# A mixture-of-experts kernel: the last quad of each expert stage written out behind the loops, and its combination spread over four PSUM banks

## The reference

```python
for i in range(2):
    if i < 1: h = h + short_conv_mixer(rmsnorm(h, norm_mix_g[i]), ...)
    else:     h = h + mla_mixer(rmsnorm(h, norm_mix_g[i]), ..., *shared_kv_side(h, ...))
    h = h + hier_moe(rmsnorm(h, norm_ffn_g[i]), w_grp[i], w_exp[i], w_gate[i], w_up[i], w_down[i])
x = rmsnorm(h, final_norm_g)[:, 16:]
# second network: two layers of hgrn2 and sparse attention on x, each x = x + rmsnorm(y, post_norm)

def hier_moe(...):   # per token: the best of 8 groups, in it the best 2 of 8 experts, with weights
    hh = jax.nn.silu(xb @ w_gate[e]) * (xb @ w_up[e])      # 1024 -> 256
    return hh @ w_down[e]                                   # 256 -> 1024; times weight, summed over both
```

## Time and profile before

| | |
|---|---|
| median of 3 runs | 1847.31 us (1847.21 to 1848.0) |
| the profiled execution | 1850.71 us, its span 1848.9 us |
| TensorE busy | 1680.2 us (91%) |
| VectorE, ScalarE, GpSimd busy | 831.7, 653.1, 63.4 us |
| DMA | 526.4 MB, mean 285 GB/s |
| expert stage 0, stage 1 | first gate product at 138.6 and 750.3 us; last addition at 594 and 1206 us |

### The profile page before, as it was taken

The page is one execution under the profiler, slowest core; times in us unless marked ns, Lnnn a source line. Parts: engine busy times, 40 slices in busy tenths (PEclk is TensorE's granted clock), DMA queues, the critical chain, the costliest instruction groups (busy, mean ns, idle before and its releaser), DMA issues.

```text
span 1848.9 us, 31186 instructions
## 1 busy us (share of the span) xinstructions
PE 1680.2 (91%) x12410; PEld 1209.6 (65%) x12410; DVE 831.7 (45%) x1501; ACT 653.1 (35%) x1175; POOL 63.4 (3%) x58
## 2 busy tenths in 40 slices
PE   8999788887979999988887878999999999999997
PEld 8995434342435869534343433499998989999897
DVE  5652122121214754322121212279776646886663
ACT  4422111111103643211110111166557645655763
POOL 1100000000001000000000000010001110000110
PEclk9999888898989999999898889999999999999999
DMA  8669999999999324999999999935542243554232
GB/s 316 236 266 414 421 422 421 421 421 421 421 422 411 116 68 154 414 421 421 422 421 421 421 421 422 374 103 170 180 165 91 94 159 120 176 170 151 92 115 92
DMA packets 89224, 526.42 MB, mean 285 GB/s; under 512 B 10032, under 2 KB 10288, under 8 KB 39728
## 3 DMA queue, kind: packets, MB, share of 16 engines
q1 hardware_dynamic: 89136, 525.19, 72.2%
HBM read 524.10 MB, written 1.05 MB: 284 GB/s over the span
## 4 chain that ended last, share of the span: by engine, by line
PE 56%; DMA 28%; DVE 6%; SPq 6%; ACT 2%; issue 1%; DVEq 0%
DMA ring<-experts 16%; PE banks L504 13%; DMA arena<-experts 11%; PE banks L508 11%; PE banks L510 10%; PE banks L509 10%; SPq L443 6%; PE banks L702 5%; PE banks L684 3%; PE banks L720 3%; DVE arena L1606 1%; DVE hT L1731 1%; DMA ring<-dense 1%; PE banks L565 1%; ACT arena L1445 1%
## 5 line engine op out<-in xcount | busy, mean ns | idle before, releaser
L508 PE MATMUL banks<-arena_parts,ring_parts 128*128 128x256 f32 (+1 forms) x1444 | 418.3, 290 | 9.3 <-ACT arena L1157 5.1
L510 PE MATMUL banks<-arena_parts,ring_parts 128*128 128x256 f32 (+1 forms) x1444 | 409.9, 284 | 0.0
L509 PE MATMUL banks<-arena_parts,ring_parts 128*128 128x256 f32 (+1 forms) x1444 | 409.3, 283 | 0.0
L504 PEld LDWEIGHTS banks<-arena 128*128 128x128 f32 (+1 forms) x2512 | 302.4, 191 | 56.3 <-issue 43.9
L504 PE MATMUL banks<-arena 128*128 128x128 f32 (+3 forms) x2512 | 335.7, 288 | 1.9 <-ACT arena L1157 1.4
L702 PE MATMUL banks<-ring,arena 128*32 128x512 f32 x1536 | 237.2, 720 | 104.9 <-DMA ring<-experts 104.7
L1157 ACT ACTIVATE arena<-banks 128x256 f32<-128x256 f32 (+6 forms) x370 | 158.7, 455 | 396.4 <-PE banks L504 162.1
L1586 DVE TENSOR_TENSOR ring_parts<-ring,ring_parts 128x1024 fp32r<-128x1024 f32 x204 | 245.8, 1238 | 98.8 <-ACT ring_parts L1157 86.8
L508 PEld LDWEIGHTS banks<-arena_parts,ring_parts 128*128 128x128 f32 x1444 | 273.3, 189 | 17.8 <-issue 8.7
L1157 ACT ACTIVATE ring_parts<-ring 128x1024 fp32r<-128x1024 f32 x208 | 215.3, 1055 | 182.3 <-DMA ring<-dense 181.0
L509 PEld LDWEIGHTS banks<-arena_parts,ring_parts 128*128 128x128 f32 x1444 | 273.6, 189 | 0.3
(11 more groups left out here) (223 smaller groups left out, 1573.3 us busy)
## 6 DMA issues: line engine op xcount, KB each, us to landing
ring<-experts SPq DMA_DIRECT2D x192, 1024.0 KB, 26.5
arena<-experts SPq DMA_DIRECT2D x160, 1024.0 KB, 22.4
ring<-dense SPq DMA_DIRECT2D x224, 512.0 KB, 4.9
at<-experts SPq DMA_DIRECT2D x16, 1024.0 KB, 24.2
x<-experts SPq DMA_DIRECT2D x16, 1024.0 KB, 22.2
consts<-consts_in SPq DMA_DIRECT2D x1, 1414.0 KB, 13.0
vecs<-vecs_in SPq DMA_DIRECT2D x1, 1125.5 KB, 15.4
hT<-h_in SPq DMA_DIRECT2D x2, 544.0 KB, 4.4
```

The costliest lines, as they stand in the source:

```text
L504: return pe.matmul(o, lhsT, rhs, start=(k == 0), stop=(k == n - 1))
L508: pe.matmul(o, lhsT[0], rhs[0], start=(k == 0), stop=False)
L509: pe.matmul(o, lhsT[0], rhs[1], start=False, stop=False)
L510: return pe.matmul(o, lhsT[1], rhs[0], start=False, stop=(k == n - 1))
```

## The change

In both expert stages:

- TensorE's loop runs once less (7 pairs here) and the last pair of quads is written out behind it; ScalarE's and VectorE's loops run 15 times and the last quad is written out. The written-out last quad leaves out `prep(i + 2)`, `tokens(i + 2)` and `slots`.
- The combination behind the loops uses banks 6, 7, 0 and 1: product c waits for addition c - 4.
- In every combination the wait for VectorE's half of the output stands before the fifth product, no longer before the first.
- The counts that the loops read are one less; VectorE does two more operations on one value to make them.

SyncE's program is as before.

```diff
--- before.py
+++ after.py
@@ -217,7 +217,7 @@
         root = sb("root", [P, T])
         scalars = sb("scalars", [P, 3 + DC])
         eps, eps_root, eps_2, g_both = scalars[:, 0:1], scalars[:, 1:2], scalars[:, 2:3], scalars[:, 3:]
-        n_iter = sb("n_iter", [P, 4], I32)
+        n_but_one = sb("n_but_one", [P, 4], I32)
         small = {n: sb(f"{n}_bf16", [P, P], BF16) for n in ("ident", "ones", "upper", "mask")}
         chosen = sb("chosen", [P, TT, NE], BF16)
         n_last = sb("n_last", [P, 2], I32)
@@ -674,21 +674,23 @@
                         if c % 4 == 3:
                             m.then_inc(s["prep_done"], 1)
 
-                def combine(i):
+                def combine(i, banks=(6, 7)):
 
                     pe.wait_ge(s["ya_ready"], i + 1)
-                    pe.wait_ge(s["yd_ready"], i + 1)
                     pe.wait_ge(s["sw_ready"], i + 1)
                     for c in range(DC):
-                        pe.wait_ge(s["add_done"], i * DC + (c if c >= 2 else 1))
-                        pe.matmul(psum[:, 6 + c % 2, 0:T], mo_y[:, c * P:c * P + P], mo_sw[:, 0:T],
+                        if c == DC // 2:
+                            pe.wait_ge(s["yd_ready"], i + 1)
+                        pe.wait_ge(s["add_done"], i * DC + max(1, c + 2 - len(banks)))
+                        pe.matmul(psum[:, banks[c % len(banks)], 0:T], mo_y[:, c * P:c * P + P], mo_sw[:, 0:T],
                                   start=True, stop=True).then_inc(s["cmb_done"], 1)
 
                 prep(1)
                 pe.wait_ge(route["iter_ready"], layer + 1)
-                half = pe.value_load(n_iter[0:1, 2 + layer:3 + layer], min_val=QUADS // 2, max_val=QUADS * ROUNDS // 2)
-
-                def quad(i, odd):
+                pairs = pe.value_load(n_but_one[0:1, 2 + layer:3 + layer], min_val=QUADS // 2 - 1,
+                                      max_val=QUADS * ROUNDS // 2 - 1)
+
+                def quad(i, odd, last=False):
 
                     def weights(u):
                         pe.wait_ge(s[f"landed{u}"], i * 16 + 16)
@@ -702,7 +704,8 @@
                             m = pe.matmul(psum[32 * e:32 * e + 32, 3, :], mo_xs[:, k, 32 * e:32 * e + 32], w[:, e, :],
                                           start=(k == 0), stop=(k == 7), tile_position=(0, 32 * e))
                         m.then_inc(s["used"], 1)
-                    prep(i + 2)
+                    if not last:
+                        prep(i + 2)
                     pe.wait_ge(s["h_ready"], i + 1)
                     for k in range(2):
                         m = pe.transpose(psum[:, 3, k * P:k * P + P], mo_h[:, k * P:k * P + P], C("ident"))
@@ -721,10 +724,12 @@
                                               start=(k == 0), stop=(k == 1), tile_position=(0, 32 * e))
                             m.then_inc(s["used"], 1)
 
-                with pe.Fori(0, half) as pair:
+                with pe.Fori(0, pairs) as pair:
                     quad(pair * 2, False)
                     quad(pair * 2 + 1, True)
-                combine(half * 2)
+                quad(pairs * 2, False)
+                quad(pairs * 2 + 1, True, last=True)
+                combine(pairs * 2 + 2, (6, 7, 0, 1))
 
             def mla():
                 norm_sum(squares, DC, T, 5)
@@ -1226,19 +1231,25 @@
 
                 tokens(1)
                 act.wait_ge(route["iter_ready"], layer + 1)
-                n = act.value_load(n_iter[0:1, layer:layer + 1], min_val=QUADS, max_val=QUADS * ROUNDS)
-                with act.Fori(0, n) as i:
+                but_one = act.value_load(n_but_one[0:1, layer:layer + 1], min_val=QUADS - 1, max_val=QUADS * ROUNDS - 1)
+
+                def quad(i, last=False):
+
                     act.wait_ge(s["used"], i * QU + 8)
                     act.activation(mo_silu[:, :], psum[:, 3, 0:256], ACT.Silu).then_inc(s["silu_done"], 1)
-                    tokens(i + 2)
+                    if not last:
+                        tokens(i + 2)
                     act.wait_ge(s["stw_done"], i + 2)
                     copy(mo_sw[:, :], psum[:, 2, 0:TP]).then_inc(s["sw_ready"], 1)
                     act.wait_ge(s["used"], i * QU + 10)
                     copy(mo_y[:, 0:512], psum[:, 4, :]).then_inc(s["ya_ready"], 1)
 
+                with act.Fori(0, but_one) as i:
+                    quad(i)
+                quad(but_one, last=True)
                 upper(after + 1)
                 for c in range(DC):
-                    act.wait_ge(s["add_done"], n * DC + (c + 2))
+                    act.wait_ge(s["add_done"], but_one * DC + (DC + c + 2))
                     if layer:
                         square(squares[:, c, 0:SEQ], hT[:, c, META:T])
                     else:
@@ -1725,10 +1736,10 @@
                     place = place.unsqueeze(1).unsqueeze(1).to_broadcast([P, TT, 4, SLOT])
                     v.tensor_tensor(mo_st, which, place, ALU.is_equal).then_inc(s["st_ready"], 1)
 
-                def add(i, c):
-
-                    v.wait_ge(s["cmb_done"], i * DC + c + 1)
-                    v.tensor_tensor(hT[:, c, :], hT[:, c, :], psum[:, 6 + c % 2, 0:T], ALU.add).then_inc(s["add_done"], 1)
+                def add(i, c, banks=(6, 7)):
+
+                    v.wait_ge(s["cmb_done"], i * DC + (c + 1))
+                    v.tensor_tensor(hT[:, c, :], hT[:, c, :], psum[:, banks[c % len(banks)], 0:T], ALU.add).then_inc(s["add_done"], 1)
 
                 slots(0, 0)
 
@@ -1737,10 +1748,12 @@
                 red(r_n, r_gt, ALU.add)
                 ts(r_n, r_n, float(QUADS), ALU.mult)
                 ts(r_c, r_n, 0.5, ALU.mult)
-                t.link(v.tensor_copy(n_iter[:, 2 + layer:3 + layer], r_c))
-                ts(r_c, r_c, -2.0, ALU.add)
+                ts(r_c, r_c, -1.0, ALU.add)
+                t.link(v.tensor_copy(n_but_one[:, 2 + layer:3 + layer], r_c))
+                ts(r_c, r_c, -1.0, ALU.add)
                 t.link(v.tensor_copy(n_last[:, layer:layer + 1], r_c))
-                t.link(v.tensor_copy(n_iter[:, layer:layer + 1], r_n), route["iter_ready"])
+                ts(r_n, r_n, -1.0, ALU.add)
+                t.link(v.tensor_copy(n_but_one[:, layer:layer + 1], r_n), route["iter_ready"])
                 tt(r1[7], r1[7], gsum, ALU.mult)
                 t.link(v.reciprocal(pg, r1[7]))
                 tt(two, two, rep(r1[6], 8), ALU.mult)
@@ -1761,15 +1774,18 @@
                     t.link(v.tensor_copy(g_squares, rep(g_both[:, :], P)), both_gains)
                     tt(g_both[:, :], V("fing"), V("pre0"), ALU.mult)
                 v.wait_ge(route["iter_ready"], layer + 1)
-                n = v.value_load(n_iter[0:1, layer:layer + 1], min_val=QUADS, max_val=QUADS * ROUNDS)
-                with v.Fori(0, n) as i:
+                but_one = v.value_load(n_but_one[0:1, layer:layer + 1], min_val=QUADS - 1, max_val=QUADS * ROUNDS - 1)
+
+                def quad(i, first_expert, last=False):
+
                     v.wait_ge(s["st_ready"], i + 1)
                     v.wait_ge(s["stw_done"], i + 1)
-                    v.tensor_tensor(mo_stw, mo_st, rep(mo_w[:, :, bass.ds((i % QUADS) * 4, 4)], SLOT), ALU.mult)\
+                    v.tensor_tensor(mo_stw, mo_st, rep(mo_w[:, :, bass.ds(first_expert, 4)], SLOT), ALU.mult)\
                      .then_inc(s["stw_ready"], 1)
-                    v.wait_ge(s["prep_done"], i * 2 + 2)
-                    v.wait_ge(s["stw_ready"], i + 1)
-                    slots(((i + 1) % QUADS) * 4, ((i + 1) // QUADS) * SLOT)
+                    if not last:
+                        v.wait_ge(s["prep_done"], i * 2 + 2)
+                        v.wait_ge(s["stw_ready"], i + 1)
+                        slots(((i + 1) % QUADS) * 4, ((i + 1) // QUADS) * SLOT)
                     v.wait_ge(s["silu_done"], i + 1)
                     v.tensor_tensor(mo_h, mo_silu, psum[:, 3, 256:512], ALU.mult).then_inc(s["h_ready"], 1)
                     v.wait_ge(s["ht_done"], i + 1)
@@ -1779,10 +1795,13 @@
                         add(i, c)
                     v.wait_ge(s["used"], i * QU + QU)
                     v.tensor_copy(mo_y[:, 512:1024], psum[:, 5, :]).then_inc(s["yd_ready"], 1)
-                v.wait_ge(s["add_done"], n * DC + 1)
+                with v.Fori(0, but_one) as i:
+                    quad(i, (i % QUADS) * 4)
+                quad(but_one, (QUADS - 1) * 4, last=True)
+                v.wait_ge(s["add_done"], but_one * DC + (DC + 1))
                 for c in range(DC):
-                    add(n, c)
-                v.wait_ge(s["add_done"], n * DC + (DC + 1))
+                    add(but_one + 1, c, (6, 7, 0, 1))
+                v.wait_ge(s["add_done"], but_one * DC + (2 * DC + 1))
                 lower_units((CONV_UNITS, FIRST_2)[layer] + 1)
 
             def rope(x, rot, cos, sin, tmp, sem=None):
```

## The result

The changed kernel takes 1834.34 us, median of four runs (1833.3 to 1834.82), beside 1847.26 us for the kernel before (four runs, 1846.4 to 1848.0): 12.9 us less, a ratio of 0.9929 with a 95% interval of 0.9912 to 0.9947. Two later series gave 0.9933 (0.9921 to 0.9946) and 0.9942 (0.9929 to 0.9955), 12.3 and 11.5 us less. The forecast was 1834.9 us, 12.4 less.

A forecast was written before the change was run, and what follows sets the result against it. Full DMA queues bound the middle of each expert stage, TensorE and what feeds it the last quad to the norm's root; 4.29 + 1.93 + 4.29 + 1.87 = 12.4 us, 1847.3 - 12.4 = 1834.9 us, range 1833.0 to 1839.0.

The forecast's parts named there:

- Part 1: Last quad: without gathering for a quad that never runs, transposes follow h sooner, 4.29 us saved in each stage.
- The weights of the last quad: Last quad's down products: weights would still land before their earlier use, covered by 3 us at the tightest place.
- Part 2: Last combination over four banks with a later wait for VectorE's half: root 1.93 us earlier in stage 0, 1.87 in stage 1.
- ScalarE is now next: Before the next norm's root: ScalarE's splits, eight squares (3.56 us) and root table end the wait, 0.4 us behind TensorE.
- Part 3: Moved loop exits, two more VectorE operations and SyncE's shifted loads: covered by waits or idle time, costing nothing.
- the written-out code: Fetching the written-out pair while DMA queues are full: taken as 0, bounds 0 to 5 us a stage.
- Rival (c): Written-out pair and shifted second loop fetched late on a full queue: 10 us a stage, 1854.9 us; chance 0.03.
- rival (b): TensorE's new pause in the last quad halves its clock: 2 us lost in each stage, 1838.9 us; chance 0.08.
- Rival (a): Only dropping the last gathering pays; the combination's 3.8 us go into ScalarE's squares and root or VectorE's additions: 1838.7; chance 0.12.
- Rival (d): The shift is given back later, by loads or attention's half-clock stretches; about 3 us left, 1844.3 us; chance 0.04.
- The other fifteen can't be won: Expert stage's quads before the last: TensorE waits for weights there, so work removed only lengthens a wait, saving nothing.
- The margin that was named but not followed: ScalarE's split behind the last quad, stage 0: fourth dense half landed at 584.6 us, wanted at 586.1.

The follow-up runs named there:

- e8: Changed kernel, plus the last quad's own combination on four banks with its first two products ahead of the transposes of h: 1832.04 us, ratio 0.9917.
- e5: Changed kernel with the wait for VectorE's output half back before the first product of every combination; last combination still on four banks: 1837.21 us, one execution.
- e6: Changed kernel with the last combination back on two banks, the wait for VectorE's half still before the fifth product: 1836.8 us, one execution.
- e3: Kernel before with only the four-bank last combination and the later wait for VectorE's half; loops and gathering as before: ratio 0.9965.
- e4: Last quads written out but keeping all their work, last combination on two banks, early wait, against the kernel before: 1850.14 against 1847.77 us, ratio 1.0014.
- e11: e4 once more, against the kernel before: 1850.93 against 1847.11 us, ratio 1.0020.
- part 1 with it: Last quads written out without the gathering, last combination on two banks, early wait, against the kernel before: 1838.67 against 1847.77 us, ratio 0.9954.
- e10: The kernel before, unchanged, profiled once more: span 1846.0 us; last Silu to root 24.03 and 23.82 us.
- e7: Changed kernel gathering only the first of three token tiles in every quad that still gathers: 1830.23 us, ratio 0.9913.

## Why the prediction was right, point by point

**Part 1 (4.29 us a stage).** Measured 4.39 and 4.22 alone. The transposes start 0.06 us behind h (574.62 + 0.42 = 575.04, 575.10), not 0.20: that pause behind VectorE's copy at 588.69 was a poor measure for the new one, and made the term 0.1 too small. The rest of the step is as worked out.

**The weights of the last quad.** Line 723 waits for no DMA in the last quad, in either stage; the cover held. e8 uses 1.8 us more of it without a wait.

**Part 2 (1.93 and 1.87).** Measured 2.11 and 2.10 alone; 1.01 of it is the banks and 1.07 the earlier start (e5 and e6, stage 0). From the start of the eight products to that of the norm's sums it is 3.77 us (584.14 to 587.91), where the forecast had 3.7, and TensorE does not pause between them.

**"ScalarE is now next": wrong.** The root waits for TensorE, with ScalarE standing 0.75 us. The term that was mis-sized is the eight squares: 3.56 forecast, 2.67 measured. The forecast took a merged row, four squares in 1.77 us, for four back to back. But VectorE's additions came in pairs then, and the group held short waits for them; the last two of the four squares had to wait for this row of the kernel before:

```profile
591.66 0.90 DVE L1731 TENSOR_TENSOR hT<-hT,banks 128x272 f32<-128x272 f32 x2 [0.43 <-PE banks L684]
```

The first row, two squares in 0.71, had the pace: about 0.3 from start to start. The rows at 586.84 (2.67 for eight) and in e3 and e8 (2.65) show it. The Trainium skill, "ScalarE: Activation LUTs", What ACT_TABLE_LOAD costs, gives 186 ns and 0.833 ns an element for an instruction with immediate scale and bias, and an overlap of about 93 ns back to back. By these figures 412 - 93 = 320 ns from start to start and eight in 2.65 us, an estimate; these rows agree.

With TensorE as the bound, as the part before worked out (2.2 us earlier, less the 0.1 by which the products start later than assumed), part 2 is 2.1 us a stage, and the sum 8.6 + 4.2 = 12.8 and not 12.4; with part 1's missing 0.1 a stage it is 13.0, against 12.9 in the distances. (A slip of 0.05 is in the forecast too: 594.82 + 1.5 is 596.32, not 596.37.)

**Part 3 and the written-out code: nothing, in the profile.** The exits are covered and the two more operations of VectorE are not seen. The code is fetched in two packets of 16 KB from 545 to 590 us (before, none), on full queues, with no pause:

```profile
q8 instruction: 2, 0.03, 0.3%
```

By the medians of e4 and e11, writing out alone has a price of 2.4 and 3.8 us. That is outside the forecast's 0 and inside the bounds it gave. It doesn't fit with the sum: with it, the whole change should give 9 to 10.5 us by the distances, and three series gave 11.5 to 12.9; part 2 without it gave 2.1 more than its distances, part 1 with it 0.5 more. In the profiles, 1.2 to 1.6 us of it stand at one burst of dense loads in the second block, where the changed kernel itself took 0.1 to 1.0 us more than the 308.0 of the kernels with the loops as they were. What e4 pays for, and whether the change pays it, stays open. It was not tried to place the loop elsewhere in the code with nothing else changed. Rival (c), 10 us a stage, is out with both series.

**The clock, rival (b): no.** Around the new pause the granted clock is 1.00, that is 2.4 GHz, in stage 1 (1176.5 to 1180.5 us) as in stage 0, whose row is (busy times of the engines, then clock, DMA share and GB/s):

```profile
573.00:577.00 4.00, 2.90 (x20) 1.30 (x12) 1.67 (x4) 0.38 (x1) 0.00 (x0) 1.00 1.00 417
```

**Rival (a)** is refuted by e3 and by 17.57 against 19.65. **Rival (d)**: the shift is carried. The two roots come 6.5 and 14.6 us earlier than before, the second 2.2 more than forecast, but that holds what the middle stretch scatters by; against e10 it is 13.4.

**"The other fifteen can't be won": too broad.** Quad 14's gathering comes after its last weights and is on the path (e7: 3.6 us less in stage 0, where 3.7 us of it are left out). For quads 0 to 13 the sentence holds, by the Silu of quad 14 in e7.

**The margin that was named but not followed.** The prediction had the fourth dense half landed 1.5 us ahead of its use. In the profile of the changed kernel it landed at 584.1 us, and ScalarE's fourth split was due at about 585.9: 1.8 us of cover in stage 0. In stage 1 it landed 11.6 us behind the last Silu and was due 11.7 behind it, so the cover is used up there already. It is what e7 and e8 ran out of, and it is the next bound of this place.

**How much of it was luck.** The mechanism of the gain is the one that was forecast, but for the engine that ends the wait before the root. The terms of its sum missed by at most 0.25 us each, most of them on the small side. That the median came out within 0.6 us is more than the medians can promise: the same kernel gave 1834.3, 1835.5 and 1835.6 us in three series, and the price of e4 was put at 0.

## What to carry to other kernels

At the end of a stage whose middle is bound by transfers there is a tail bound by the engines; work for a step still to come was free in the middle (over 50 us of it in e7, at most 1 us gained), but in the tail work for a step that never comes costs a full distance, which is not its own duration but that to the next input that is ready (4.4 us for 5.6 us of products). A merged row of a timeline can hide waits: take an engine's pace from the shortest stretch of the same instruction. And a chain that has been shortened by 2 us meets transfers that have not moved, so the order of what waits for them (split, then square) has to be looked at again.

## What the runs showed of the hardware

The kernel scatters by 2 to 3 us between executions, in the attention and the second block, and in part by the last halves of short bursts of dense loads: they took 6.6 to 9.1 us where a half takes 4.9 in the median, at places that recur from execution to execution. A median of five can't tell 2 us, and two series gave writing out a price of 2.4 and 3.8 us of which the profiles show a part, at one such burst (ScalarE's wait for it 2.70 and 2.45 us for 0.6 to 0.7). But a stretch between two instructions in one profile repeats to 0.03 us where only the engines set it, which is what the terms of the change were told apart by. A pause of 0.96 us did not lower TensorE's clock in the last quads (1.00 from 573 to 577 us and from 1176.5 to 1180.5).
